# A two-block transformer stack on one core: the hand-written order of the second mixer, with pairs 1 to 3 a chunk earlier, the compressed attention moved, and the weights cast one chunk less ahead

## The reference

```python
x = x + 0.5 * swiglu(rms_norm(x, g1), w_gate, w_up, w_down)      # d_ff = 2816
x = x + mixer(rms_norm(x, g2))                                   # first or second kind
x = x + 0.5 * swiglu(rms_norm(x, g3), w_gate, w_up, w_down)
```

```python
q, kv, gates, moba = split(h @ w_in)
kc = gelu(blocks(k_cmp + pos) @ w_ck1) @ w_ck2      # 15 overlapping blocks of 32 tokens
vc = gelu(blocks(v_cmp + pos) @ w_cv1) @ w_cv2
o_cmp = softmax(q @ kc, masked) @ vc                # compressed attention
o_slc, o_win = causal attention of rope(q) on rope(k_slc), rope(k_win)
o_nsa = g0 * o_cmp + g1 * o_slc + g2 * o_win        # 8 heads of 64, g = sigmoid(gates)
o_moba = causal attention of 8 more heads
y = concat(o_nsa, o_moba) @ w_out
```

## Time and profile before

| | us |
|---|---|
| median of 3 runs (2121.52 to 2121.72) | 2121.6 |
| the profiled execution's own time | 2121.6 |
| its span, first to last instruction | 2119.8 |
| PE busy | 2078.1 (98%) |
| POOL busy | 1583.8 (75%) |
| ACT busy | 1084.9 (51%) |
| DVE busy | 793.1 (37%) |

### The profile page before, as it was taken

How to read it: one execution, slowest core, us unless ns; L and a number is a source line. 1 busy time by engine, 2 the same in 40 slices (tenths; PEclk the granted TensorE clock), 3 DMA queues, 4 the chain that set the end, 5 groups by cost and what they waited for, 6 DMA issues and landing times.

```text
span 2119.8 us, 35566 instructions
## 1 busy us (share of the span) xinstructions
PE 2078.1 (98%) x12488; PEld 1787.1 (84%) x12488; DVE 793.1 (37%) x1762; ACT 1084.9 (51%) x1873; POOL 1583.8 (75%) x670
## 2 busy tenths in 40 slices
PE   8999999999999999999999999899999999989998
PEld 7888998888888898888888888688888889868887
DVE  2224644223322564322332256532233225553223
ACT  5445535545554554544545467454455446745444
POOL 7887846888888775688888883468888888346886
PEclk9999999999999999999999999999999999989999
DMA  6555433555455443455545553445555555244553
GB/s 244 189 186 182 170 130 129 189 184 191 178 189 181 171 169 126 144 187 188 195 172 188 184 177 110 169 139 187 189 189 178 181 189 180 100 169 140 189 188 117
DMA packets 101139, 363.44 MB, mean 171 GB/s; under 512 B 11840, under 2 KB 12480, under 8 KB 100928
## 3 DMA queue, kind: packets, MB, share of 16 engines
q1 hardware_dynamic: 100624, 361.02, 48.9%
q10 hardware_dynamic: 432, 1.28, 0.2%
HBM read 361.21 MB, written 1.05 MB: 171 GB/s over the span
## 4 chain that ended last, share of the span: by engine, by line
PE 96%; DVE 2%; ACT 1%; issue 1%; DMA 0%; ACTq 0%; SPq 0%; DVEq 0%; POOLq 0%
PE twin L583 30%; PE twin L587 19%; PE twin L645 9%; PE twin L647 9%; PE twin L646 9%; PE twin L585 5%; PE twin L586 4%; PE twin L700 1%; PE twin L757 1%; PE twin L629 1%; PE twin L630 1%; PE twin L631 1%; PE twin L763 1%; PE twin L774 1%; PE twin L1081 1%
## 5 line engine op out<-in xcount | busy, mean ns | idle before, releaser
L553 POOL TENSOR_TENSOR wlo<-raw,whi 128x1024 fp32r<-128x1024 f32 x666 | 1583.6, 2407 | 520.6 <-ACT whi L1250 520.3
L1250 ACT CAST whi<-raw 128x1024 fp32r<-128x1024 f32 x666 | 679.5, 1051 | 96.1 <-PE twin L647 49.1
L587 PE MATMUL twin<-turned,wlo 128*128 128x256 f32 x1968 | 554.3, 282 | 0.0
L583 PE MATMUL twin<-turned,whi 128*128 128x512 f32 x1344 | 480.3, 400 | 1.2 <-DVE turned L1622 1.2
L583 PE MATMUL twin<-early,whi 128*128 128x512 f32 x1344 | 479.9, 398 | 0.5
L587 PE MATMUL twin<-early,wlo 128*128 128x256 f32 x1536 | 431.3, 281 | 0.0
L1682 DVE TENSOR_TENSOR twin<-twin,mix 128x512 f32<-128x512 f32 x168 | 117.4, 699 | 758.1 <-ACT mix L1309 758.1
L587 PEld LDWEIGHTS twin<-turned,wlo 128*128 128x128 f32 x1968 | 374.2, 190 | 3.3
L1309 ACT COPY mix<-twin 128x512 f32<-128x512 f32 x168 | 98.5, 587 | 439.2 <-PE twin L587 439.2
L583 PEld LDWEIGHTS twin<-turned,whi 128*128 128x128 f32 x1344 | 253.2, 188 | 63.8 <-issue 1.6
L583 PEld LDWEIGHTS twin<-early,whi 128*128 128x128 f32 x1344 | 252.5, 188 | 64.1 <-issue 2.0
(11 more groups left out here) (283 smaller groups left out, 2133.6 us busy)
## 6 DMA issues: line engine op xcount, KB each, us to landing
raw<-in_w_dram SPq DMA_DIRECT2D x682, 512.0 KB, 3.2
con<-in_con_dram ACTq DMA_DIRECT2D x1, 1177.5 KB, 7.6
x<-in_x_dram SPq DMA_DIRECT2D x2, 512.0 KB, 7.5
out_dram<-xs SPq DMA_DIRECT2D x4, 256.0 KB, 2.8
mix<-in_last_gain_dram SPq DMA_DIRECT2D x1, 512.0 KB, 5.1
par<-in_par_dram SPq DMA_DIRECT2D x2, 208.0 KB, 3.2
par<-in_par_dram SPq DMA_DIRECT2D x2, 154.0 KB, 3.1
con<-in_con_dram ACTq DMA_DIRECT2D x1, 64.0 KB, 3.8
```

What stands on the lines that cost most here:

```text
L553: nc.gpsimd.tensor_tensor(wlo[:, place, :], raw[:, place, :], whi[:, place, :].bitcast(F32), ALU.subtract).then_inc(split_done, 1)
L583: pe.matmul(out, hi, both.rearrange("p c n -> p (c n)"), start=start and k == 0, stop=False, skip_group_check=True)
L587: mm = pe.matmul(out[:, 0:SEQ], lo, both[:, 0, :], start=False, stop=stop and k == KD - 1, skip_group_check=True)
L1250: nc.scalar.copy(whi[:, place, :], raw[:, place, :]).then_inc(hi_done, 1)
```

## The change

It edits the tables of the second mixer's order and three places of ACT's loop:

- `SCORED`: pairs 1, 2 and 3 are scored at chunks 9, 10, 11 instead of 10, 11, 12. With them their transposes (11, 12, 13 instead of 12, 13, 14) and weightings (12, 13, 14 instead of 13, 14, 15) move. Pairs 0 and 4 to 9 stay; pair 11 is weighted at 29 instead of 30.
- `ROTATE`: M3 is rotated at chunk 21 instead of 23; the other entries come out the same.
- `KC_DONE` 26 to 27, `CMP_SCORED` 28 to 29, `CMP_TURNED` 32 to 31.
- `SKIPS` of the second mixer: 8, 14, 22 instead of 4, 13, 19.
- `taken(Q1)` is the first step of ACT's chunk 11 instead of the last.
- The cast is always four slots ahead; before, it was five ahead from chunk 20 on.

```diff
-ROTATE = {LAST[m] + {KSW: 4, Q0: 3, M3: 3}.get(m, 1): m for m in ROPED}
+ROTATE = {LAST[m] + 1 + (4 if m == KSW else 3 if m == Q0 else 1) - 1: m for m in ROPED}
...
-SCORED = {8: 0, 10: 1, 11: 2, 12: 3, 13: 4, 14: 5, 15: 6, 16: 7, 17: 8, 19: 9, 21: 10, 25: 11}
+SCORED = {8: 0, 9: 1, 10: 2, 11: 3, 13: 4, 14: 5, 15: 6, 16: 7, 17: 8, 19: 9, 21: 10, 25: 11}
 TURNED = {c + (4 if p == 10 else 2): p for c, p in SCORED.items()}
-WEIGHED = {c + (3 if p >= 10 else 1): p for c, p in TURNED.items()}
-GATES_TURNED, HID0_TURNED, KC_DONE, CMP_SCORED, CMP_TURNED = 7, 25, 26, 28, 32
+WEIGHED = {c + (3 if p == 10 else 2 if p == 11 else 1): p for c, p in TURNED.items()}
+GATES_TURNED, HID0_TURNED, KC_DONE, CMP_SCORED, CMP_TURNED = 7, 25, 27, 29, 31
...
-SKIPS = {MIX1: (8, 14, 20, 26), MIX2: (4, 13, 19)}
+SKIPS = {MIX1: (8, 14, 20, 26), MIX2: (8, 14, 22)}
...
                 for c in range(MIX2):
                     for m in TAKEN.get(c, ()):
-                        if m != Q1:
-                            taken(m)
+                        taken(m)
                     if c - 1 in SCORED:
                         pair_normal(SCORED[c - 1])
-                    ahead = AHEAD + (c >= LAST[M3])
-                    if c >= AHEAD and c + ahead < MIX2 + AHEAD and FFN_SLOTS + c + ahead not in L.whole:
-                        split_hi(L, FFN_SLOTS + c + ahead)
+                    if c >= AHEAD and FFN_SLOTS + c + AHEAD not in L.whole:
+                        split_hi(L, FFN_SLOTS + c + AHEAD)
                     if c in WEIGHED and sums_end(WEIGHED[c]):
                         sums_kept(WEIGHED[c])
                     if c in SCORED:
                         pair_exps(SCORED[c])
-                    if c == LAST[Q1] + 1:
-                        taken(Q1)
```

## The result

The changed kernel takes 2133.4 us (median of five executions, 2128.2 to 2137.2), the kernel before 2121.6 (median of five, 2117.4 to 2122.2). The ratio is 1.0058, 95% interval [1.0042, 1.0075]. Measured again on another chip, the same kernel took 2134.4 and a ratio of 1.0067 [1.0053, 1.0081]. It is slower by about 12 us. The forecast was 2127.5 with a range up to 2133. The profiled execution takes 2130.8, with a span of 2129.0, so it is 2.6 us faster than the median.

What follows compares the result with a forecast made beforehand. PE, busy 98% of the span, was taken as the bound. Filled part +11.5, chunks 21 to 25 +1.0 and chunks 27 to 32 -6.6 gave +5.9 us on 2121.6: 2127.5, range 2120.5 to 2133.

Steps and rivals of the forecast that it cites:

- Both cost nothing: Moved skip places and cast one less ahead: no cost, as long as GpSimd's queue is empty by chunk 14.
- falls again at times ... I take 1.0: Chunks 27 to 32 after the change: low clock costs 1.0 us per run, bounds 0 and 3.5.
- The filled part: Chunks 5 to 20, without PE waits before: new waits of 5.75 us per run, +11.5 for two.
- the 3.8 that chunks 27 to 32 were to give back: Clock term of both runs in chunks 27 to 32: 5.8 us removed against 2.0 put there.
- my -5.6: Both runs from chunk 21 on: +1.0 us for chunks 21 to 25 and -6.6 for chunks 27 to 32.
- slower, clock in full: Clock falls in chunks 27 to 32, reaching output chunks behind the 4.0 wait: +2.5 us per run, 2132.5, chance 0.14.
- Chunks 9, 10 and 15: PE waits for banks at the scores: 0.7, 0.85 and 0.75 us per run.
- Chunks 12 and 13, `taken(Q1)`: Q1's copy early on ScalarE: PE waits 0.95 us for pair 2's probabilities, 2.5 for bank 4.
- Chunks 21 and 25: PE waits 2.2 us at M3's rotation, then 0.55: 2.75 against 2.22 per run, +1.0 for two.
- The step that took 4.0 for both runs: At the turn of compressed probabilities, GpSimd's lo half 36 blocks VectorE line 2177: PE waits 4.0 us per run.
- the other case: Line 2177 slips in before lo half 36: PE waits 1.75 us per run, +1.4 in all, 2123, chance 0.28.
- The clock that was to be won there: Half clock at the first output chunks removed: 2.3 us in the first run, 2.3 plus 1.2 in the second.

Runs made afterwards that it cites:

- end_only: Kernel before with only pair 11 weighted at 29, keys at 27, compressed scores at 29, cast always four ahead, turn still at 32: 2113.6 us, ratio 0.9966.
- pairs_back: Changed kernel with pairs 1 to 3 scored at chunks 10 to 12 and the copy of Q1's bank last again: 2118.5 us.
- Before_filled: Kernel before with 20 thrown-away 128x512 matmuls in the wait ahead of the first output chunk: 2118.0 us, ratio 0.9985.

## Why the direction was right, and where the prediction failed

The direction was right (slower), and so was the balance: a queue in chunks 9 to 15 that costs more than chunks 27 to 32 give back. The time was 5.9 us too low, just past the range: half of the loss. Two steps failed.

1. **"Both cost nothing", of the skip places and of the cast one less ahead.** I asked whether PE would miss a lo half. I didn't ask what stands behind the cast on ScalarE. For the skip places, waits of 1.96 per run came from there, 3.9 in all; the skipped places put back gave 5.0. Of the difference between the 7.10 measured and my 5.75 it is more than the whole: the rest was 5.14, a little under my sum. The cast one less ahead isn't free either: 0.95 per run in end_only. In the changed kernel, with M3's rotation in chunk 21, that wait doesn't appear, and the 0.59 that does was in my sum.
2. **The clock.** It was priced only in chunks 27 to 32 ("falls again at times ... I take 1.0"), as 5.8 removed against 2.0 put there. The filled part, with clock 1.00 in the earlier trace rows, got no such term. But its new waits let the clock fall in some executions, with dense work behind each of them. And the 3.8 that chunks 27 to 32 were to give back don't show in the profile: PE is busy for 0.6 us more than before (2078.7, 2078.1) with the same matmuls.

The forecast was for the profiled execution, which got slower by 9.2. Its sums, forecast and measured, for both runs of the mixer:

| | forecast | measured |
|---|---|---|
| waits in the filled part | +11.5 | +14.2 |
| waits from chunk 21 on | -1.7 | -5.4 |
| clock (measured: PE's busy time) | -3.8 | +0.6 |
| in all | +5.9 | +9.2 |
| the median beyond the profiled execution | 0 | +2.6 |

(The sums are off by 0.1 and 0.2, since waits under 0.3 us are left out and the terms are rounded.) So the loose part came out near my -5.6 by luck: its waits fell by 3.7 more than I had forecast, most of it where the multiply slipped in and PE waited 1.70, and the clock gave back none of its 3.8.

The last row is likely the clock of the filled part. By medians the moved pairs and the copy of Q1 cost 15.0, of which 11.8 are waits (14.2 less the 2.4 that pairs_back keeps). The 3.2 left over are a remainder and not a measurement of the clock, but filling five waits gave back 3.6, and the changed kernel measured again shows the falls. Which of these waits matter stays open: filling that of chunk 13 alone gave nothing, moving the rotation gave nothing, and filling all five did. My rival "slower, clock in full" had the size and put it behind the wait at line 1165. The clock does fall there in the profile (0.89 and 0.72 above), but that profile is faster than the median.

Point by point:

- Chunks 9, 10 and 15: 0.7, 0.85 and 0.75 forecast. The pairs alone gave 0.70, 0.66 and 0.69. With the skip places it is 1.42, 0.90 and 1.69.
- Chunks 12 and 13, `taken(Q1)`: 0.95 and 2.5 forecast, 0.67 and 2.42 measured, the latter ended by ScalarE's copy of the sums (line 1500), as written down.
- Chunks 21 and 25: 2.2 and 0.55 forecast, 2.20 and 0.59 measured. My later expectation that the old place would bring back 2.22 was wrong: it has 3.17, and end_only shows the later cast as the reason.
- Chunks 27 to 32: bank 4 0.36 (0.55 forecast), bank 6 0.79 (1.2), line 1165 1.70 and 3.78 in one execution, 3.79 twice in another (4.0). The step that took 4.0 for both runs was too strong, and the chance of 0.28 for the other case too low: six of 16 slipped in. Shown by holding GpSimd back: 1.70 and 1.75.
- The clock that was to be won there, 2.3 and 3.5 us: filling the wait of the kernel before gave 3.4 of these 5.8 by medians, and 6.2 between the two profiled executions. The output chunks behind it do run at full clock then; why the median moved less isn't traced.
- Line 2171 lasts 2.00 while GpSimd works and line 2173 takes 0.42 or 2.51, by who was first. The rule of the Trainium skill ("SBUF — State Buffer", under "SBUF: two separate sides", the shared port pair as an exclusive lock) agrees with that. Which of the two would start first I had to assume, and I took GpSimd both times.
- With matmuls in the wait of the kernel before, the stretches around it have clock 1.00, where without them it is 0.61 and 0.54 (the two rows shown with the clock). The Trainium skill ("TensorE: Matmul & The Clock Gate", under "What's actually happening") has the slow state as the default, which activity releases. Before_filled agrees.

## What to carry to other kernels

A cast or copy that is in time for its own reader can still be too early in its engine's order: if it has to wait, everything behind it waits, so check each moved buffer place against what is queued behind the instruction that fills it. In a stretch without idle time, price a new wait above its length: PE's clock may fall behind it, as it did here in some executions, and then the dense work behind runs at half speed until it is back. Try the parts of such an edit apart; here the end by itself was a gain of 7 us that its company turned into a loss of 12.

## What the runs showed of the hardware

- The same kernel with the same waits of PE before chunk 27 had spans of 2129.0 and 2136.2 us, with PE busy for 2078.7 and 2085.3, by where the granted clock fell. Behind a wait of 2.42 us four small matmuls took 0.65 in one execution and 1.12 in the other.
- The same mean clock costs two kernels different amounts. Each 0.001 less goes with 0.5 to 0.9 us in the kernel before (70 executions: 2120.9 at 0.995, 2121.4 at 0.994, 2122.3 at 0.993) and with some 2.5 in the changed one (14: 2130.0 at 0.996, 2135.1 at 0.994).
- A multiply of 0.42 us on VectorE lasts about 2.51 when GpSimd's next instruction is first. In the 24 cases of twelve profiles, who is first goes with the time at which the cast for that instruction ended. Twelve times it ended between 0.04 us before the end of VectorE's preceding line and 0.94 behind it, and VectorE was first. Twelve times it ended 0.12 to 1.50 us before, and GpSimd was. The same program has it both ways in one execution.
- Not only products of two SBUF tiles seem to be held up: line 2168, which reads one SBUF tile and constants, lasts 0.95 and ends at 1369.70, 2.43 us behind the start of GpSimd's row of three (7.44 in all), which is about where the first of the three ends. The sum over the same tile (0.42) and the reciprocal (0.25) beside it are not held up.
